# A ring of eight weight halves with lo written over raw, and stage ends run token tile by token tile

## The reference, cut to what matters

```
def rmsnorm(x, gain): return x * rsqrt(mean(x * x, -1) + 1e-6) * gain
def swiglu(h, w_gate, w_up, w_down): return (silu(h @ w_gate) * (h @ w_up)) @ w_down

x = x + 0.5 * rmsnorm(swiglu(rmsnorm(x, ffn1_pre_g), gate1, up1, down1), ffn1_post_g)
q, f_logit, i, g, u = split(rmsnorm(x, mix_pre_g) @ w_in)     # w_in is 2048 x 5120
y = concat(hgrn2_mixer(q, f_logit, i, g, ...), pool_mixer(u, ...)) @ w_out
x = x + rmsnorm(y, mix_post_g)
x = x + 0.5 * rmsnorm(swiglu(rmsnorm(x, ffn2_pre_g), gate2, up2, down2), ffn2_post_g)
```

## Time and profile before

| | us |
|---|---|
| runs | 1876.82, 1878.26, 1879.60 (median 1878.26) |
| profiled execution, first to last instruction | 1875.8 |
| TensorE busy | 1837.3 (98%) |
| VectorE busy | 951.9 (51%) |
| ScalarE busy | 804.5 (43%) |
| GpSimd busy | 49.6 (3%) |
| DMA, weight queue | 339.77 MB, 55.4% of 16 engines |

### The profile page before, as it was taken

How to read it: one execution, slowest core, us unless ns; L and a number is a source line. 1 busy time by engine, 2 the same in 40 slices (tenths; PEclk the granted TensorE clock), 3 DMA queues, 4 the chain that set the end, 5 groups by cost and what they waited for, 6 DMA issues and landing times.

```text
span 1875.8 us, 21635 instructions
## 1 busy us (share of the span) xinstructions
PE 1837.3 (98%) x8386; PEld 1525.8 (81%) x8386; DVE 951.9 (51%) x965; ACT 804.5 (43%) x926; POOL 49.6 (3%) x110
## 2 busy tenths in 40 slices
PE   7999999999999999999999999999999999999997
PEld 6888888888788887788888877888888888788886
DVE  4544445544444444655745456445444544444544
ACT  5444444444433434643234445444444444433432
POOL 0000000000000000250000000000000000000000
PEclk9999999999999999999999999999999999999998
DMA  7665656556566656455443554555555655555552
GB/s 263 189 198 180 196 183 192 188 186 194 194 198 191 197 186 199 158 184 176 135 135 131 200 185 149 188 191 189 183 197 182 198 179 191 208 185 201 186 194 90
DMA packets 145438, 344.68 MB, mean 184 GB/s; under 512 B 5400, under 2 KB 5472, under 8 KB 145008
## 3 DMA queue, kind: packets, MB, share of 16 engines
q1 hardware_dynamic: 144544, 339.77, 55.4%
q0 software_dynamic: 736, 4.26, 0.6%
q10 hardware_dynamic: 112, 0.03, 0.0%
HBM read 341.94 MB, written 2.10 MB: 183 GB/s over the span
## 4 chain that ended last, share of the span: by engine, by line
PE 97%; DVE 1%; ACT 1%; POOL 0%; issue 0%; DMA 0%; DVEq 0%; SPq 0%; POOLq 0%; ACTq 0%; PEldq 0%
PE ps L729 31%; PE ps L731 31%; PE ps L730 31%; PE ps L801 1%; PE ps L891 1%; PE ps L783 1%; DVE x L562 0%; PE ps L928 0%; ACT ps L311 0%; DMA x<-in_x_dram 0%; POOL hrr L282 0%; PE ps L918 0%; PE ps L879 0%; DVE xT_lo L488 0%; ACT xT_hi L318 0%
## 5 line engine op out<-in xcount | busy, mean ns | idle before, releaser
L481 DVE TENSOR_TENSOR wlo<-raw,whi 128x1024 fp32r<-128x1024 f32 x640 | 783.0, 1226 | 844.3 <-ACT whi L299 840.3
L299 ACT ACTIVATE whi<-raw 128x1024 fp32r<-128x1024 f32 x640 | 677.7, 1060 | 919.8 <-PE ps L731 918.8
L729 PE MATMUL ps<-whi,xT_hi 128*128 128x512 f32 x1728 | 680.5, 394 | 6.7 <-DVE wlo L481 4.4
L731 PE MATMUL ps<-whi,xT_lo 128*128 128x512 f32 x1728 | 674.9, 391 | 0.0
L730 PE MATMUL ps<-wlo,xT_hi 128*128 128x512 f32 x1728 | 674.6, 390 | 0.0
L729 PEld LDWEIGHTS ps<-whi,xT_hi 128*128 128x128 f32 x1728 | 325.8, 189 | 73.8 <-issue 4.8
L731 PEld LDWEIGHTS ps<-whi,xT_lo 128*128 128x128 f32 x1728 | 325.7, 188 | 68.7
L730 PEld LDWEIGHTS ps<-wlo,xT_hi 128*128 128x128 f32 x1728 | 326.1, 189 | 66.1
L729 PE MATMUL ps<-whi,hT_hi 128*128 128x512 f32 x832 | 324.5, 390 | 2.0 <-PEq L936 1.6
L731 PE MATMUL ps<-whi,hT_lo 128*128 128x512 f32 x832 | 323.7, 389 | 0.0
L730 PE MATMUL ps<-wlo,hT_hi 128*128 128x512 f32 x832 | 323.7, 389 | 0.0
(11 more groups left out here) (99 smaller groups left out, 365.7 us busy)
## 6 DMA issues: line engine op xcount, KB each, us to landing
raw<-in_ffn_w_gate_dram SPq DMA_DIRECT2D x88, 1024.0 KB, 5.2
raw<-in_ffn_w_up_dram SPq DMA_DIRECT2D x88, 1024.0 KB, 5.2
raw<-in_ffn_w_down_dram SPq DMA_DIRECT2D x88, 1024.0 KB, 5.2
raw<-in_w_in_dram SPq DMA_DIRECT2D x40, 1024.0 KB, 5.1
raw<-in_w_out_dram SPq DMA_DIRECT2D x16, 1024.0 KB, 4.9
x<-in_x_dram SPq DMA_DIRECT2D x4, 512.0 KB, 9.3
gpost<-in_ffn_post_g_dram POOLq DMA_DIRECT2D x2, 1024.0 KB, 5.0
out_dram<-x SPq DMA_DIRECT2D x4, 512.0 KB, 2.9
```

Source lines behind the costliest of these rows:

```text
L299: nc.scalar.activation(whi[:, g % RING, :], raw[:, g // 2 % RAW, 1024 * (g % 2):1024 * (g % 2 + 1)], ACT.Copy).then_inc(hi_ready, 1)
L481: V.tensor_tensor(wlo[:, g % RING, :], raw[:, g // 2 % RAW, 1024 * (g % 2):1024 * (g % 2 + 1)], whi[:, g % RING, :].bitcast(f32), ALU.subt ...
L729: mm(bank, a_hi, whi[:, s, c0:c0 + NT], start=start, stop=False)
L731: return mm(bank, a_lo, whi[:, s, c0:c0 + NT], start=False, stop=stop)
```

## The change

- **Ring.** `RING` is 8 and `AHEAD` 5. `wlo` lies over `raw`, so that `lo` is written in place. A load waits for `w_used` of the pair eight halves back; a cast waits for its load alone.
- **Wide stages** start with two halves on banks 0 and 1 and then the same two on banks 2 and 3 (`wide_start`), in both passes. The second pass ends with four halves run bank by bank: token tile 0's two banks, then token tile 1's (`wide_split`).
- **Narrow stages after a boundary** (IN, U2) begin with the same shape: halves 0 to 3 for token tile 0, then for token tile 1 (`first_halves`).
- **Norms, residuals and transposes** go by units, one token tile by 512 columns, in the order `UNITS`. A unit is four transposes into one bank, four casts and four subtractions of 128 x 128. The root is taken for one token tile at a time, and the factor 0.5 is folded into the mean (`over`).
- **The last hidden tile** is transposed after three halves of the down stage, on all engines.
- **The end** has two stores of 512 KB for token tile 0 and four of 256 KB for token tile 1.
- `yg` is eight tiles at scattered places, `gpost` moves to 176 KB. The down stages' two passes are written out and not looped on TensorE.

```diff
-RING = 4
-AHEAD = RING - 1
+RING = 2 * RAW
+AHEAD = 5
+SPLIT = 4
+UNITS = ((0, 0), (0, 1), (1, 0), (1, 1), (0, 2), (1, 2), (0, 3), (1, 3))
...
     raw = at("raw", 0, [P, RAW, 2048])
+    wlo = at("wlo", 0, [P, RING, 1024], f32r)
     whi = at("whi", 32, [P, RING, 1024], f32r)
-    wlo = at("wlo", 48, [P, RING, 1024], f32r)
...
-                if not (isinstance(j, int) and first_half + 16 * j < 2 * RAW):
-                    sp.wait_ge(lo_ready, j * 16 + (first_half - 2 * RAW + 2))
+                if not (isinstance(j, int) and first_half + 16 * j < RING):
+                    sp.wait_ge(w_used, j * 16 + (first_half - RING + 2))
...
-            for n in range(DN):
-                sp.wait_ge(xn_ok, TOK * DN * 2 + TOK * (n + 1))
-                sp.dma_start(ov[:, :, n * NT:(n + 1) * NT], x[:, :, n * NT:(n + 1) * NT]).then_inc(out_ok, 16)
-            sp.wait_ge(out_ok, 16 * DN)
+            stores = [(0, 0, 2), (0, 2, 2)] + [(1, n, 1) for n in range(DN)]
+            for t, n, w in stores:
+                sp.wait_ge(xn_ok, TOK * DN * 2 + DN * t + n + w)
+                sp.dma_start(ov[:, t, n * NT:(n + w) * NT], x[:, t, n * NT:(n + w) * NT]).then_inc(out_ok, 16)
+            sp.wait_ge(out_ok, 16 * len(stores))
...
+            def inv_root(n, k, t0=0, t1=TOK):
+                pool.wait_ge(ms_ok, n)
+                nc.gpsimd.tensor_tensor(rr[:, k, t0:t1], ms[:, k, t0:t1], mhalf[:, t0:t1], ALU.pow).then_inc(r_ok, 1)
...
-                if not (isinstance(j, int) and g + 16 * j < RING):
-                    act.wait_ge(w_used, j * 16 + (g - RING + 1))
...
+            def unit_hi(step, g0, u):
+                t, n = UNITS[u]
+                act.wait_ge(u_tr, 8 * (step - 1) + u + 1)
+                act.wait_ge(xn_ok, 8 * (step - 1) + {0: 2, 4: 6, 6: 8}.get(u, u + 1))
+                for c in range(4):
+                    k = 4 * n + c
+                    ins = nc.scalar.activation(xT_hi[:, k, t * P:(t + 1) * P], ps[TB[u % 3]][:, c * P:(c + 1) * P],
+                                               ACT.Copy, scale=vcol[:, g0 + k:g0 + k + 1])
+                ins.then_inc(u_hi, 1)
...
+            def pair_last(k, d, b, between):
+                hi(b + 1)
+                    for n in range(2):
+                        if t and n:
+                            act.wait_ge(w_used, b)
+                        else:
+                            act.wait_ge(y_done, 4 * d + 2 + 2 * t + n)
+                        y_square(k, 1, t, n)
+                        between(t, n)
+            def boundary(d, k, b, g0):
+                def between(t, n):
+                    if (t, n) == (0, 1):
+                        hi(b + 2)
+                    if (t, n) == (1, 0):
+                        unit_hi(d + 1, g0, 0)
+                        hi(b + 3)
+                pair_last(k, d, b, between)
+                unit_hi(d + 1, g0, 1)
+                unit_hi(d + 1, g0, 2)
+                unit_hi(d + 1, g0, 3)
+                hi(b + 4)
+                unit_hi(d + 1, g0, 4)
+                unit_square(k + 1, d + 1, 0)
+                unit_square(k + 1, d + 1, 1)
+                unit_hi(d + 1, g0, 5)
+                hi(b + 5)
...
+                hi(b + 8)
...
+            def unit_lo(step, g0, u):
+                t, n = UNITS[u]
+                dve.wait_ge(u_hi, 8 * (step - 1) + u + 1)
+                for c in range(4):
+                    k = 4 * n + c
+                    ins = V.scalar_tensor_tensor(out=xT_lo[:, k, t * P:(t + 1) * P], in0=ps[TB[u % 3]][:, c * P:(c + 1) * P],
+                                                 scalar=vcol[:, g0 + k:g0 + k + 1],
+                                                 in1=xT_hi[:, k, t * P:(t + 1) * P].bitcast(f32),
+                                                 op0=ALU.mult, op1=ALU.subtract)
+                    if c % 2:
+                        ins.then_inc(u_lo, 1)
...
+                link(V.tensor_reduce(out=ms[:, k, t0:t1], in_=ss[:, k, t0:t1, :], op=ALU.add, axis=AX.X))
+                V.tensor_scalar(ms[:, k, t0:t1], ms[:, k, t0:t1], over / D, over * EPS,
+                                ALU.mult, ALU.add).then_inc(ms_ok, 1)
...
+            def boundary(d, k, b, g0):
+                def unit(u):
+                    residual(k, *UNITS[u])
+                lo(b + 1)
+                last_gain(d, 0, 0)
+                last_gain(d, 0, 1)
+                token_root(d, k, 0)
+                dve.wait_ge(y_free, 8 * d + 6)
+                dve.wait_ge(r_ok, 3 * d + 2)
+                unit(0)
+                unit(1)
+                last_gain(d, 1, 0)
+                lo(b + 2)
+                unit_lo(d + 1, g0, 0)
+                lo(b + 3)
+                last_gain(d, 1, 1)
+                token_root(d, k, 1)
+                unit_lo(d + 1, g0, 1)
+                dve.wait_ge(y_free, 8 * d + 8)
+                dve.wait_ge(r_ok, 3 * d + 3)
+                unit(2)
+                unit(3)
+                unit_lo(d + 1, g0, 2)
+                unit(4)
+                unit_lo(d + 1, g0, 3)
+                unit(5)
+                lo(b + 4)
+                unit_lo(d + 1, g0, 4)
+                unit(6)
+                unit_lo(d + 1, g0, 5)
+                unit(7)
+                lo(b + 5)
+                unit_lo(d + 1, g0, 6)
+                lo(b + 6)
+                unit_lo(d + 1, g0, 7)
+                lo(b + 7)
+                lo(b + 8)
+            def tail(d, k):
+                last_gain(d, 0, 0)
+                last_gain(d, 0, 1)
+                    token_root(d, k, t)
+                    dve.wait_ge(y_free, 8 * d + 6 + 2 * t)
+                    dve.wait_ge(r_ok, 3 * d + 2 + t)
+                    for n in range(DN):
+                        residual(k, t, n)
+                    if t == 0:
+                        last_gain(d, 1, 0)
+                        last_gain(d, 1, 1)
...
+            def wide_start(b, order, a_hi, a_lo, ready):
+                for n in range(2):
+                    ready(n)
+                    for h in range(2):
+                        if n == 0:
+                            pe.wait_ge(lo_ready, b + h + 1)
+                        for t in range(TOK):
+                            ins = wide(b + h, n, t, order[h], a_hi, a_lo, start=h == 0)
+                        if n:
+                            ins.then_inc(w_used, 1)
...
+            def wide_split(b, order, a_hi, a_lo, between=None):
+                last = len(order) - 1
+                for t in range(TOK):
+                    for n in range(2):
+                        for h in range(last - SPLIT + 1, last + 1):
+                            if between and t and n and h == last - SPLIT + 2:
+                                between()
+                            if not t and not n:
+                                pe.wait_ge(lo_ready, b + h + 1)
+                            ins = wide(b + h, n, t, order[h], a_hi, a_lo, stop=h == last)
+                            if t and n:
+                                ins.then_inc(w_used, 1)
+                        if not (t and n):
+                            ins.then_inc(y_done, 1)
...
+            def transpose_unit(step, u):
+                t, n = UNITS[u]
+                pe.wait_ge(xn_ok, 8 * (step - 1) + u + 1)
+                if 8 * (step - 1) + u >= 3:
+                    pe.wait_ge(u_lo, 16 * (step - 1) + 2 * (u - 2))
+                for c in range(4):
+                    k = 4 * n + c
+                    ins = nc.tensor.transpose(ps[TB[u % 3]][:, c * P:(c + 1) * P], x[:, t, k * P:(k + 1) * P], ident[:])
+                ins.then_inc(u_tr, 1)
...
+            def first_halves(b, d):
+                step = d + 1
+                transpose_unit(step, 1)
+                for t in range(TOK):
+                    pe.wait_ge(y_free, 8 * d + 5 + 2 * t)
+                    for h in range(SPLIT):
+                        if (t, h) in ((1, 0), (1, 1), (1, 2)):
+                            transpose_unit(step, h + 3)
+                        pe.wait_ge(u_lo, 16 * (step - 1) + 4 * t + h + 1)
+                        if t == 0:
+                            pe.wait_ge(lo_ready, b + h + 1)
+                        for c in range(2):
+                            k = 2 * h + c
+                            if (t, h, c) == (0, 2, 1):
+                                transpose_unit(step, 2)
+                            ins = three(ps[t][:], xT_hi[:, k, t * P:(t + 1) * P], xT_lo[:, k, t * P:(t + 1) * P],
+                                        (b + h) % RING, c * NT, k == 0, False)
+                        if t:
+                            ins.then_inc(w_used, 1)
...
+            def rest_of_units(step, h):
+                if h == SPLIT:
+                    transpose_unit(step, 6)
+                if h == SPLIT + 1:
+                    transpose_unit(step, 7)
+                pe.wait_ge(u_lo, 16 * (step - 1) + 4 * (h // 2) + 3 + h % 2)
...
+                wide_start(b, order, hT_hi, hT_lo, ready)
```

(61 more changed lines are left out.)

248 lines of the change are left out of this document (133 added, 115 removed).

## The result

The changed kernel takes 1855.42 us (median of 4 runs, 1854.74 to 1855.81), against 1878.93 for the kernel before beside it on the same chip (1876.82 to 1879.77): ratio 0.9877, 95% interval 0.9865 to 0.9889. Forecast were 1858.7 and a range of 1854 to 1866. The span went from 1875.8 to 1853.7; the forecast span was 1856.2. Each experiment's time stands beside 1877.45 to 1878.35 for the kernel before; ratios are against it. The experiments ran on three chips, and between these the kernel before itself differed by 0.9 us (by 1.5 from the result's), so differences of about 1 us between experiments are read from the stages in their traces and not from the medians.

A forecast was written before the change was run, and what follows sets the result against it. TensorE, busy 98% of 1875.8 us, bounds the kernel; only removing its waits pays. Terms -5.7 - 4.9 - 5.3 - 0.9 - 3.3 + 0.5 = -19.6 give span 1856.2, plus 2.5 makes 1858.7 us; range 1854 to 1866.

The forecast's parts named there:

- Two of the forecast's signs: TensorE goes from up to down without a gap; the span ends 8.4 to 8.9 us after the last matmul.
- Up to down: Up to down, with mixer to output: transposes moved behind three halves remove the waits, -5.3 us, bounds -5.3 to -4.
- Level steps: Mixer's level steps: copies start about 1.3 us later against their matmuls, TensorE does not wait; 0, bounds 0 to +3.
- Boundaries: Ends of first down stage and output projection: each still loses 3.0 us, so gains are 5.7 and 4.9 us.
- rival A: Both boundaries: each 128-column operation costs what a 256 one does, 3.5 us more each, 1865.7 us; chance 0.15.
- Rivals C: Mixer's level steps stall: landings above 6 us cost 3 to 5 us in all, 1862.5 us; chance 0.06.
- D: Split does nothing: units come so late that both boundaries keep their whole 6 us and clock, 1869.3 us; chance 0.03.
- Rival B: Boundaries: several waits count as idleness and the clock still falls, +2 to +3 us each, 1863.5 us; chance 0.12.
- Start: Program start: five halves, not three, stand on both engines before x part 2; +0.5 us, bounds 0 to +2.
- pairs: Between column pairs of a wide stage: the new order removes 0.3 us three times, -0.9 us.
- tail: After the last matmul: shorter chain of norms and residuals -3.0 us, smaller last store -0.3, sum -3.3.
- Rival E: Every pair's load in the stages comes late on w_used, from a landing of 14 us; 1890 us at 14.1; chance 0.04.

The follow-up runs named there:

- the ring alone: Kernel before with only the change's ring (RING 8, AHEAD 5, loads on w_used, down passes written out), stage ends as before: 1886.63 us, ratio 1.0043.
- the later loads: Changed kernel with every load released two halves later, w_used of 2n - 4 and not 2n - 6 for pair n: 2040.66 us in one execution.

## Why the prediction was right, and where its terms were off

**The mechanism held.** The boundaries' long waits and their stretch at 1.2 GHz ended, the stages' joints closed but for the wait below, and the tail shortened; steady tiles kept 44.43 us. The sum was 2.5 us short, and that it came so near is partly luck: up to down and the start brought 2.3 less than forecast, the other places 4.8 more. Two of the forecast's signs did not come: there is a wait between up and down, and the span ends 7.9 us after the last matmul's end (8.15 after its start), not 8.4 to 8.9.

**Up to down, mis-sized by 2.0.** The one step that failed is "Banks 2 and 3 come free at: last matmul's signal +0.2, two gate products 1.4, 1.7 us in all". It counted the products and not what stands ahead of them in VectorE's program. With AHEAD at 5 that is the subtraction of the half five past the tile's last, whose load is released when TensorE is done with all but the tile's last two halves, 5.4 us before the stage's end (issued at 500.86). Its cast starts 5.2 later, at 506.09, the subtraction at 507.18, and the products at 508.32. So banks 2 and 3 came free 3.9 us after the last matmul's start, where the forecast had 1.7 from its end and 2.72 would have hidden them. The experiment that moved one subtraction gave back 2.1 us in the trace. The reasoning had been made for the level steps ("stands behind lo(p+4)") and not applied here.

**Level steps, right.** The level matmuls end at 889.80 and the copies start 1.1 us after that, where before they started at once (897.35 in the earlier trace rows, matmuls until 897.3); TensorE takes the next level on time all the same:

```profile
890.94 2.46 DVE L715 COPY_PREDICATED S<-mask,ps 128x128 f32<-128x128 int32 x8
...
897.90 1.33 PE L1080 MATMUL ps<-qP,kR 128*128 128x64 f32 x11
```

897.90 is the 905.42 of the earlier trace rows less the 7.52 gained so far. Forecast was 1.3, and no wait. (The forecast's own terms add up to 898.6 and not 898.7.)

**The mixer's end, missed.** Its 0.72 come with the ring alone. In the kernel before, TensorE waits there once, for VectorE's `orn` (L672), before the first small matmul on `band`, which starts 0.81 after the matmul ahead of it:

```profile
995.68 0.39 PE L731 MATMUL ps<-whi,xT_lo 128*128 128x512 f32 x1
996.49 0.70 PE L918 MATMUL ps<-band,u_sb 128*128 128x256 f32 x2 [0.42 <-DVE orn L672]
```

After the change the same matmul starts 0.23 after its forerunner (988.16 to 988.39), and VectorE was done 1.0 us before. Why VectorE is further ahead there was not isolated.

**Boundaries: a loss of 3.0 forecast, 1.9 measured.** The gains were 7.1 and 6.3 where 5.7 and 4.9 were forecast: 1.1 each from the smaller loss after, and about 0.3 each because the loss before was 9.0 and 8.3, not 8.7 and 7.9. A unit of four operations spans 1.12 on VectorE, as interpolated, and 1.14 on ScalarE, not 1.20. Grouped by line, the two unit operations:

```profile
L341 ACT ACTIVATE xT_hi<-ps,vcol 128x128 fp32r<-128x128 f32 x64 | 18.2, 370 | 12.4 <-PE ps L916 10.4 <-DVE x L621 1.9
L554 DVE SCALAR_TENSOR_TENSOR xT_lo<-ps,vcol,xT_hi 128x128 fp32r<-128x128 f32 x64 | 18.0, 344 | 6.6 <-ACT xT_hi L341 6.3
```

Four start 0.26 apart on both engines ((1.12 - 0.34) / 3 and (1.14 - 0.37) / 3). The Trainium skill (VectorE: DVE Perf Modes, section on the TRN2 errata) gives formulas for PSUM sources, by which the estimate is 0.26 on VectorE and 0.25 on ScalarE; the trace agrees. Its warning of small tiles, rival A, did not decide, since an operation of 128 columns does not cost what one of 256 does (0.26 apart, against (1.66 - 0.48) / 3 = 0.39 on VectorE in the earlier trace rows, with 0.48 the mean duration of one). The forecast lists five waits, which add up to 2.4 and not 2.5. Three came, at 0.15, 0.36 and 0.5 (forecast 0.5, 0.4, 0.9), 1.0 in all; the first transposes and unit 5's residual did not wait. The other 0.9 of the loss is the step to the second matmul behind each wait and each group of transposes, 0.31 to 0.34 in place of 0.23, some ten times at a boundary. Rivals C and D did not come either (level steps 0.00; both boundaries shorter). Rival B fell with the waits: none reached 0.6 us at a boundary or 1.0 elsewhere behind the first tile, and the clock did not fall before the last matmul.

**Start, pairs and tail, small terms.** The start's +0.78 is one execution against one; with the deeper ring and the order of the change the first eight halves take 27.26 to 27.76 in six, against 26.80 before, so the +0.5 of the forecast holds within what such a comparison can tell. A pair gave 0.48, not 0.3: behind the 0.53 of the earlier trace rows the next matmul started 0.34 later, another 0.11 over the ordinary 0.23. In the tail the chain of norms gave 3.2 (3.0 forecast; the root on 128x1 is 0.54, not 0.71) and the store 0.7 (0.3). Its size explains 0.47 of that. By the Trainium skill (DMA: Bandwidth & Descriptors, Anatomy of one DMA), whose fit is for GpSimd's path, the difference of the two sizes is an estimate of 0.6; the trace has 0.5 on SyncE's queue.

**Outside the span** there are 1.8 us (1855.5 against 1853.7, and 1.7 to 1.9 in every execution profiled here), not the 2.5 that the forecast added: the profiled execution of before was 0.7 faster than its median. This 0.7 and the 2.5 of the sum make up the 3.2, of the 3.3 between forecast and median.

**Rival E's threshold was wrong by its mechanism.** It gave a pair 8.8 us of cover, counted to the pair's own use. Loads 5.4 us later should then have cost nothing in steady stages; they cost 1.1 a tile there and 185 us in all. The cover that counts is that of the side work written behind each subtraction, and by the forecast's own estimate 0.8 was left of it at the level steps; at the gate products none was. The rival did not happen in the changed kernel, whose loads landed in 5.1 to 5.2, but its chance of 0.04 stood on the wrong number.

## What to carry to other kernels

When engines run their programs in order, a deeper lookahead puts side work behind younger loads: for each operation that TensorE waits for, find the weight step ahead of it, that step's load and the event that releases the load. Split a stage's end by token tile so that one's norm lies beside the other's matmuls: here split and small tiles together left a loss of 1.9 us of 9.0 and 8.3. Moving an operation out of one engine's queue can delay the partner engine's: walk both programs before moving it.

## What the runs showed of the hardware that was not expected

- TensorE kept 2.4 GHz where two starts stood 1.18 (after), 2.00 (before) or 2.08 us apart (the ring alone, and once with the later loads), and fell to 1.2 GHz behind starts 3.73 and 3.87 us apart (the ring alone), for 3.4 and 6.8 us, and once behind starts 2.91 us apart (the later loads), for 3.4 us.
- The root on GpSimd takes 0.56 us on 128x1 and 0.71 on 128x2 (means of six each).
- At 2.4 GHz a matmul after a wait has a duration of 0.50, not 0.39, and the next starts 0.34 later, not 0.23: each wait costs 0.11 more than it lasts.
